# Ranks, places and silu in the routed experts of a two-layer trunk step on one core

## The chip, the cores and the metric

The kernel runs on one core of a Trainium2 chip, as one launch. The metric is the device time in microseconds (us) from start to end, as the median of three runs.

## The reference, cut to what matters

The reference is one step of a trunk of 2 layers on 384 tokens (128 of context, 256 latent) of width 1024. Each layer has a mixer (gated recurrence and three attentions) and then a routed feed-forward part. The change touches only that second part:

```python
def hier_moe(h, w_rg, w_re, w_g, w_u, w_d):
    glog = (x @ w_rg)                       # 4 group logits per token
    gsel = argmax(glog)                     # one group
    gw = softmax(glog)[gsel]
    elog_g = (x @ w_re)[..., gsel, :]       # 4 experts of that group
    top_p, top_i = top_k(softmax(elog_g), 2)
    top_p = top_p / sum(top_p)
    gate = one_hot(gsel * 4 + top_i) * (gw * top_p)
    hid = silu(x @ w_g) * (x @ w_u)         # 16 experts, 1024 -> 256
    y = (hid * gate) @ w_d                  # 256 -> 1024
```

All is float32.

## The kernel before, in words

**How a product is made.** The weights come from memory in units of 128 x 1024 floats (512 KB) that SyncE's queue loads. Each float32 product is made of three matmuls on rounded halves (line 1389 to 1391: high by high, low by high, high by low). So for each unit ScalarE makes the high half (`whi`, lines 1002 and 1010), VectorE in the experts or GpSimd in the mixer makes the low half (`wlo`, lines 1927 and 854), and TensorE then runs 6 matmuls of 512 columns. Three buffers (`CONV` = 3) of halves turn round: ScalarE may convert unit n only when TensorE has done with unit n - 3. Twelve raw buffers (`RING`) lie in front of that.

**The experts.** A token goes to one group, and its group's experts are run on tiles of 128 tokens, sorted by group through a table in memory. There are 6 tiles in a layer (`NT`), each with the 24 units (`UNITS`) of its group's four experts. For expert e, units (e, 0) to (e, 3) hold the gate and up weights and give `G`; then ScalarE takes tanh of the gate part (line 1297), and VectorE's `hidden` makes (tanh + 1) x gate part (line 2327) and multiplies by the token's routing weight and the up part (line 2331; the factor 2 of this form of silu is taken out of the weight in `route`). TensorE turns the result (line 1801), ScalarE and VectorE make its halves (`ehi`, `elo`), and units (e, 4), (e, 5) are the down projection into `S`. At the end of a tile ScalarE copies `S` to `yo` (line 1325). In tile 0 the rows of the tile are not read from memory but selected by matmul (line 1851) with a 0/1 matrix `sel` from the normalised rows `hn`. GpSimd scatters all rows to the sorted table (line 924), reads the next tile's rows (`hs`, line 940) and TensorE turns them (line 1809) after unit 18. TensorE's and VectorE's code of tiles 1 to 4 is a loop in hardware, and so is ScalarE's for tiles 0 to 4.

**The route.** `route` (line 576) is VectorE's part. After the router's logits it picks the group (`rg_dve`), and TensorE counts with two small matmuls (line 1566) each token's rank in its group and the groups' sizes (`rc_pe`). VectorE makes `sel` from that, finishes `hn` (`whole_row`), and then, between low halves of tile 0's units (`unit_low`, `rows_low`), it works out, in this order: the best two experts (`rt_dve`, to ScalarE's Exp on line 1291, back with `rt_act`), the routing weights (`gates_dve`, to the matmul on line 1831), the places in the sorted table (lines 647 to 663, `slot_dve`, to GpSimd's scatter). `tables`, run after unit 8 of tile 0, makes the numbers of the weight blocks of the last two tiles and the matrix of the last tile's places.

**TensorE around the route.** In layer 0 it also makes part of the next layer's modulation from 8 blocks, in two quads of 32 matmuls (`quad`, lines 1346 to 1352): one ahead of the ranks' matmuls and one behind. `keep_busy` issues matmuls on the identity that nothing reads (line 1446): `BUSY_RANK` of them ahead of the ranks' matmuls, `BUSY_PLACE` behind, each a pair of numbers for the two layers. Engines run their queues in order; semaphores join them.

Of the kernel before, what the change touches and what calls it, by code (L numbers as in the profile page):

```python
# [24 lines left out]
ALU = mybir.AluOpType  # L25
ACT = mybir.ActivationFunctionType
AX = mybir.AxisListType.X
# [70 lines left out]
BUSY_RANK, BUSY_PLACE = (0, 12), (11, 24)  # L98
NLOG = 20
SELECT_GATES = 3  # L100
# [189 lines left out]
def program(nc, a, out, counts):  # L290
# [4 lines left out]
    with ctx:  # L295
# [193 lines left out]
        e_tanh, e_dve, e_hid, e_pt = sg("e_tanh"), sg("e_dve"), sg("e_hid", credit=2), sg("e_pt")  # L489
# [86 lines left out]
        def route(dve, need, own, tt, whole_row, rows_low, next_mods, unit_low):  # L576
# [44 lines left out]
            for n in (1, 2):  # L621
                unit_low(n)

            prod = rw[:, :, 32:48].rearrange("p t (g e) -> p t g e", g=4)
            own(tt(prod, el.rearrange("p t (g e) -> p t g e", g=4), gsel.unsqueeze(3).to_broadcast([P, TILES, 4, 4]), ALU.mult))
            own(V.tensor_reduce(rw[:, :, 28:32], prod.rearrange("p t g e -> p t e g"), AX, ALU.add))
            rows_low(0)
            eg = rw[:, :, 28:32]
            first_max(eg, m1, sel1)
            own(V.tensor_scalar(rw[:, :, 48:52], sel1, NEG, None, ALU.mult))  # L630
            own(tt(rw[:, :, 48:52], rw[:, :, 48:52], eg, ALU.add))
            first_max(rw[:, :, 48:52], m2, sel2)
            rt_dve.of(tt(rw[:, :, 12:13], m2, m1, ALU.subtract))
            rows_low(1)
            unit_low(CONV)
            need(rt_act, 0)

            own(V.tensor_reduce(rw[:, :, 14:15], rw[:, :, 0:4], AX, ALU.add))
            own(V.tensor_scalar(rw[:, :, 15:16], rw[:, :, 4:5], 1.0, 2.0, ALU.add, ALU.mult))
            own(tt(rw[:, :, 14:15], rw[:, :, 14:15], rw[:, :, 15:16], ALU.mult))  # L640
            own(V.reciprocal(rw[:, :, 15:16], rw[:, :, 14:15]))
            own(tt(sel2, sel2, b4(rw[:, :, 4:5]), ALU.mult))
            own(tt(sel1, sel1, sel2, ALU.add))
            gates_dve.of(tt(hn[:, :, D:ROW], sel1, b4(rw[:, :, 15:16]), ALU.mult))
            unit_low(CONV + 1)
# [16 lines left out]
            own(V.tensor_scalar(rw[:, :, 13:14], slot, float(-(NT - 1) * P), None, ALU.add))  # L662
            slot_dve.of(V.tensor_scalar(slot_at[:, :].unsqueeze(2), slot, -1.0, None, ALU.add))
            need(sg_pe, 0)
            q_gate.of(V.tensor_copy(gate[:, :], O[:, 0:GRP]))
            for n in range(CONV + 2, LEAD):
                unit_low(n)
            next_mods()

            def tables():  # L670

                own(V.tensor_scalar(first, order[:, 4:4 + OVER], base[:, 1:2], None, ALU.is_ge))
# [6 lines left out]

                for t in range(TILES):  # L680
                    ins = V.tensor_scalar(sel[:, t, :], order[:, 4 + NT:4 + NT + P], rw[:, t, 13:14], None, ALU.is_equal)
                sel_dve.of(ins)

            return tables
# [140 lines left out]
        def _(pool):  # L825
# [9 lines left out]
            for l in range(layers):  # L835
# [30 lines left out]
                for s in SCHEDULE:  # L866
# [52 lines left out]
                    elif s == ("route",):  # L919
                        need(zero_out, NT)  # L920
                        pool.wait_ge(*slot_dve.at(l, 0))
                        carry()
# [52 lines left out]
        def _(act):  # L975
# [8 lines left out]
            for l in range(layers):  # L984
# [52 lines left out]
                for s in SCHEDULE:  # L1037
# [247 lines left out]
                    elif s == ("route",):  # L1285
# [4 lines left out]
                        act.wait_ge(*rt_dve.at(l, 0))  # L1290
                        rt_act.of(nc.scalar.activation(rw[:, :, 0:5], rw[:, :, 8:13], ACT.Exp))
                        rows_high(1, 0)
                    elif s == ("experts",):
                        def one_tile(i, last):
                            def tanh(e):
                                act.wait_ge(*e_unit.in_tile(l, i, UT, GATED[e]))
                                e_tanh.of(nc.scalar.activation(gact[:, e % 2, :], G[:, e % 2, 0:DEXP], ACT.Tanh, scale=0.5))
# [6 lines left out]
                            for n in range(3, UT):  # L1304
                                if n - 3 in GATED:
                                    tanh(GATED.index(n - 3))
                                high(i, n)
# [1230 lines left out]
```

## Time and profile before

| | |
|---|---|
| median of 3 runs | 1696.46 us (1696.36 to 1699.31) |
| profiled execution | 1698.88 us, its span 1697.3 us |
| TensorE busy | 1660.7 us, 98% |
| VectorE busy | 1010.2 us, 60% |
| ScalarE busy | 858.6 us, 51% |
| GpSimd busy | 647.4 us, 38% |
| experts of layer 0, layer 1 (us of the span) | from about 619 and 1453 |

Busy shares are means over the whole program. TensorE's ends are modelled, so its 98% holds small gaps; they are seen in the starts of the matmuls.

### The profile page before, as it was taken

What the parts mean: (1) busy time and instruction counts of PE and PEld (TensorE: products, weight loads), DVE (VectorE), ACT (ScalarE), POOL (GpSimd) and SP (SyncE); (2) the same over time, 40 slices, a digit from 0 to 9 for tenths busy, and PEclk for the clock granted to TensorE, in tenths of its full rate; (3) what the DMA queues carried; (4) which work ended last, traced back from release to release, by engine and by line L of the source; (5) the groups of instructions that cost most, each with busy time, mean ns of one, the idle gap of its engine ahead of it and who ended that gap; (6) DMA issues with size and microseconds to landing.
All of it is one profiled execution on the core that took longest, in us unless ns stands there. A gap on an engine that the chain in (4) does not pass through costs nothing.

```text
span 1697.3 us, 27078 instructions
## 1 busy us (share of the span) xinstructions
PE 1660.7 (98%) x10057; PEld 1342.9 (79%) x10057; DVE 1010.2 (60%) x1710; ACT 858.6 (51%) x1452; POOL 647.4 (38%) x408
## 2 busy tenths in 40 slices
PE   8999999999999999999999999999999999899998
PEld 7788887777888877777778888777788888777776
DVE  3137577563450279999851384765535314899997
ACT  2443344444532347878644334554544333487884
POOL 0644463434476621101135555543346674110102
PEclk9999999999999999999999999999999999999999
DMA  9723344253656659999865334334344654799994
GB/s 350 264 87 109 106 149 137 94 181 137 210 205 231 236 198 401 371 369 367 301 231 194 100 115 131 122 121 149 131 181 153 258 208 140 279 383 365 373 366 152
DMA packets 128110, 367.21 MB, mean 216 GB/s; under 512 B 12028, under 2 KB 42364, under 8 KB 128000
## 3 DMA queue, kind: packets, MB, share of 16 engines
q1 hardware_dynamic: 93872, 319.80, 52.3%
q10 hardware_dynamic: 27504, 21.74, 4.1%
q0 software_dynamic: 6624, 24.18, 3.8%
q8 instruction: 72, 1.18, 0.3%
q14 instruction: 38, 0.31, 0.1%
HBM read 341.71 MB, written 23.97 MB: 215 GB/s over the span
## 4 chain that ended last, share of the span: by engine, by line
PE 73%; DVE 13%; issue 5%; ACT 4%; DMA 2%; POOL 1%; SPq 1%; ACTq 0%; DVEq 0%; POOLq 0%
PE G L1389 19%; PE G L1391 17%; PE G L1390 17%; DVE wlo L1927 5%; ACT whi L1010 3%; DVE pA L1927 2%; PE T L1714 2%; PE O L1465 2%; PE O L1745 2%; PE S L1700 2%; DMA x_scratch<-pA 2%; PE S L1389 1%; DVE prob L1927 1%; PE T L1618 1%; PE S L1391 1%
## 5 line engine op out<-in xcount | busy, mean ns | idle before, releaser
L854 POOL TENSOR_TENSOR wlo<-raw,whi 128x1024 fp32r<-128x1024 f32 x198 | 488.3, 2471 | 557.5 <-ACT whi L1002 557.3
L1389 PE MATMUL G<-whi,hhi 128*128 128x512 f32 (+1 forms) x1440 | 578.7, 402 | 12.3 <-DVE wlo L1927 6.2
L1391 PE MATMUL G<-whi,hlo 128*128 128x512 f32 (+1 forms) x1440 | 557.9, 387 | 0.0
L1390 PE MATMUL G<-wlo,hhi 128*128 128x512 f32 (+1 forms) x1440 | 557.4, 387 | 0.0
L1389 PEld LDWEIGHTS G<-whi,hhi 128*128 128x128 f32 x1440 | 270.5, 188 | 91.0 <-DVE wlo L1927 21.1
L1391 PEld LDWEIGHTS G<-whi,hlo 128*128 128x128 f32 x1440 | 270.4, 188 | 57.4
L1390 PEld LDWEIGHTS G<-wlo,hhi 128*128 128x128 f32 x1440 | 271.1, 188 | 46.8
L1002 ACT ACTIVATE whi<-raw 128x1024 fp32r<-128x1024 f32 x204 | 214.7, 1054 | 99.6 <-PE G L1391 66.3
L1927 DVE TENSOR_TENSOR wlo<-raw,whi 128x1024 fp32r<-128x1024 f32 x150 | 179.7, 1220 | 6.7 <-ACT whi L1010 3.6
L1010 ACT ACTIVATE whi<-raw 128x1024 fp32r<-128x1024 f32 x144 | 152.7, 1060 | 40.7 <-PE G L1391 26.8
L1927 DVE TENSOR_TENSOR wlo<-pA,whi 128x1024 fp32r<-128x1024 f32 x72 | 88.0, 1224 | 33.2 <-ACT whi L1010 31.7
L1010 ACT ACTIVATE whi<-pA 128x1024 fp32r<-128x1024 f32 x72 | 76.5, 1063 | 36.3 <-PE S L1391 18.7
L1927 DVE TENSOR_TENSOR wlo<-pB,whi 128x1024 fp32r<-128x1024 f32 x72 | 85.6, 1224 | 7.4 <-ACT whi L1010 6.8
L1229 ACT ACTIVATE prob<-prob,am 128x384 f32<-128x384 f32 x64 | 38.9, 609 | 99.3 <-DVE am L1927 52.9
L1389 PE MATMUL S<-whi,ehi 128*128 128x512 f32 x192 | 79.4, 414 | 6.3 <-DVE elo L1927 5.9
L1010 ACT ACTIVATE whi<-pB 128x1024 fp32r<-128x1024 f32 x72 | 75.0, 1056 | 7.7 <-PE G L1391 7.1
L1389 PE MATMUL G<-whi,bhi 128*128 128x512 f32 x192 | 78.4, 408 | 0.0
L849 POOL TENSOR_TENSOR sink_col<-ones 128x1 f32<-128x1 f32 x26 | 15.7, 603 | 162.4 <-ACT yo L1325 76.7
L1391 PE MATMUL S<-whi,elo 128*128 128x512 f32 x192 | 75.4, 392 | 0.0
L1390 PE MATMUL S<-wlo,ehi 128*128 128x512 f32 x192 | 75.1, 391 | 0.0
L1391 PE MATMUL G<-whi,blo 128*128 128x512 f32 x192 | 75.1, 391 | 0.0
L1390 PE MATMUL G<-wlo,bhi 128*128 128x512 f32 x192 | 74.9, 390 | 0.0
(404 smaller groups left out, 2323.3 us busy)
## 6 DMA issues: line engine op xcount, KB each, us to landing
raw<-in_units SPq DMA_DIRECT2D x423, 512.0 KB, 5.1
pA<-in_units SPq DMA_DIRECT2D x78, 512.0 KB, 5.8
pB<-in_units SPq DMA_DIRECT2D x72, 512.0 KB, 5.9
h_sorted<-sig POOLq DMA_DIRECT2D x12, 514.0 KB, 6.9
hs<-h_sorted POOLq DMA_DIRECT2D x10, 514.0 KB, 7.4
y_sorted<-yo POOLq DMA_DIRECT2D x10, 512.0 KB, 7.0
bias<-in_nat_bias ACTq DMA_DIRECT2D x16, 256.0 KB, 3.6
pB<-rows_scratch ACTq DMA_DIRECT2D x8, 512.0 KB, 9.2
```

The lines of the kernel that those rows point to most:

```text
L854: lo_done.of(nc.gpsimd.tensor_tensor(wlo[:, k, :], raw[:, POS_OF[g] % RAW, :], whi[:, k, :].bitcast(F32), ALU.subtract))
L1002: hi_done.of(nc.scalar.activation(whi[:, g % CONV, :], raw[:, p % RAW, :], ACT.Copy))
L1010: hi_done.of(nc.scalar.activation(whi[:, n % CONV, :], expert_raw(n), ACT.Copy))
L1229: e = nc.scalar.activation(prob[:, u % 2, m, lo:lo + w], src, ACT.Exp, bias=am[:, u % 2, i:i + 1], accum_out=am[:, u % 2, 4 + i:5 + i])
L1389: nc.tensor.matmul(dst, st_hi, mv_hi, start=start, stop=False)
L1390: nc.tensor.matmul(dst, st_hi, mv_lo, start=False, stop=False)
L1391: return nc.tensor.matmul(dst, st_lo, mv_hi, start=False, stop=stop)
L1465: mm = nc.tensor.matmul(O[32 * q:32 * q + 32, c0:c0 + P], cond[:, k, :], raw[:, MODPOS[j - MQ + 1 + q] % RAW, k * P:(k + 1) * P], start=(k ...
L1700: nc.tensor.matmul(S[:, m, 0:256], q, kT[r, kj, 0:256], start=True, stop=True)
L1714: mm = nc.tensor.transpose(T[:, m, b * P:(b + 1) * P], prob[:, u % 2, m, b * P:(b + 1) * P], ident[:, :])
L1745: mm = nc.tensor.matmul(O[64 * m:64 * m + 64, to], values(b, lo, 64), pr, **fl)
L1927: return V.tensor_tensor(o, i0, i1, op)
```

## The change

It moves work inside the route, and takes silu in one operation of ScalarE.

```diff
-BUSY_RANK, BUSY_PLACE = (0, 12), (11, 24)
+BUSY_RANK, BUSY_PLACE = (0, 14), (0, 28)
-SELECT_GATES = 3
+SELECT_GATES = 4
+TABLES = (12, 15)
 # VectorE, route: new order after the ranks' sums, sel and whole_row(2)
-            for n in (1, 2):
-                unit_low(n)
-            (group's expert logits) rows_low(0) (best two experts, rt_dve)
-            rows_low(1) unit_low(CONV) need(rt_act, 0)
-            (routing weights, gates_dve) unit_low(CONV + 1)
             (places: at, tiles, base, diff, cum, slot; slot_dve)
+            unit_low(1) rows_low(0) unit_low(2)
+            (group's expert logits, best expert)
+            rows_low(1) unit_low(CONV)
+            (second expert, rt_dve) unit_low(CONV + 1) need(rt_act, 0)
-            own(V.tensor_scalar(rw[:, :, 15:16], rw[:, :, 4:5], 1.0, 2.0, ALU.add, ALU.mult))
+            own(V.tensor_scalar(rw[:, :, 15:16], rw[:, :, 4:5], 1.0, None, ALU.add))
+            (routing weights, gates_dve) unit_low(CONV + 2)
             need(sg_pe, 0)
             q_gate.of(V.tensor_copy(gate[:, :], O[:, 0:GRP]))
-            for n in range(CONV + 2, LEAD):
-                unit_low(n)
             next_mods()
 # tables: block numbers, now after unit 12 (with the slot offset of rw 13);
 # the last tile's matrix is split off as last_places, after unit 15
-                                if n == LAST_SEL and first:
-                                    tables()
+                                if n in TABLES and first:
+                                    finish_route[TABLES.index(n)]()
 # GpSimd, scatter of the rows
                         pool.wait_ge(*slot_dve.at(l, 0))
+                        pool.wait_ge(*gates_dve.at(l, 0))
 # ScalarE
                         rows_high(0, 0)
-                        act.wait_ge(*rt_dve.at(l, 0))
-                        rt_act.of(nc.scalar.activation(rw[:, :, 0:5], rw[:, :, 8:13], ACT.Exp))
                         rows_high(1, 0)
-                                e_tanh.of(nc.scalar.activation(..., G[:, e % 2, 0:DEXP], ACT.Tanh, scale=0.5))
+                                e_silu.of(nc.scalar.activation(..., G[:, e % 2, 0:DEXP], ACT.Silu))
                                 high(i, n)
+                                if n == CONV + 1 and first:
+                                    act.wait_ge(*rt_dve.at(l, 0))
+                                    rt_act.of(nc.scalar.activation(rw[:, :, 0:5], rw[:, :, 8:13], ACT.Exp))
-                        with act.Fori(0, NT - 1) as i:
-                            one_tile(i, False)
-                        one_tile(NT - 1, True)
+                        for i in range(NT):
+                            one_tile(i, i == NT - 1, i == 0)
 # TensorE, route
                         if l < DEPTH - 1:
-                            quad(0)
+                            quad(0, range(KD // 2))
                         keep_busy(S[:, 1, 0:P], BUSY_RANK[l])
                         need(rg_dve, 0)
                         (the ranks' two matmuls, rc_pe)
                         if l < DEPTH - 1:
+                            quad(0, range(KD // 2, KD))
                             quad(1)
                         keep_busy(S[:, 1, 0:P], BUSY_PLACE[l])
 # VectorE, hidden
-                                dve.wait_ge(*e_tanh.in_tile(l, i, GRP, e))
+                                dve.wait_ge(*e_silu.in_tile(l, i, GRP, e))
-                                e_dve.of(V.scalar_tensor_tensor(ga_, ga_, 1.0, b[:, 0:DEXP], ALU.add, ALU.mult))
-                                dve.wait_ge(*e_dve.in_tile(l, i, GRP, e))
```

Lines in brackets stand for statements that are the same before and after, moved as they are. `SELECT_GATES` is the unit of tile 0 after which TensorE makes the tile's routing weights.

## Rows read from the trace of the kernel before

**Rows 1.** Windows: two stretches of the experts; busy us (x instructions) by engine, clock, DMA.

```profile
648.00:662.00 14.00, 13.69 (x65) 10.83 (x65) 13.18 (x16) 10.81 (x15) 2.29 (x3) 1.00 1.03 410
699.00:735.50 36.50, 35.91 (x161) 28.11 (x160) 33.77 (x39) 29.17 (x36) 4.30 (x6) 1.00 0.98 375
```

**Rows 2.** Chain of waits through tile 2 of layer 0: start us, us, what.

```profile
699.28 0.44 ACT yo L1325
...
710.84 0.43 DVE sig L2327
711.68 1.23 DVE wlo L1927
712.96 0.50 PE G L1389
...
735.92 0.44 ACT yo L1325
```

**Rows 3.** Timeline of TensorE in tile 2: start us, us, engine, line, operation.

```profile
712.50 0.39 PE L1391 MATMUL S<-whi,elo 128*128 128x512 f32 x1
...
730.97 0.39 PE L1390 MATMUL S<-wlo,ehi 128*128 128x512 f32 x1
731.20 0.39 PE L1391 MATMUL S<-whi,elo 128*128 128x512 f32 x1
731.91 0.49 PE L1389 MATMUL S<-whi,ehi 128*128 128x512 f32 x1 [0.32 <-DVE elo L1927]
```

**Rows 4.** Timeline of VectorE in tile 2.

```profile
731.37 0.41 DVE L1927 TENSOR_TENSOR elo<-T,ehi 128x256 fp32r<-128x256 f32 x1
```

**Rows 5.** Groups of instructions by line, ScalarE: busy, mean ns, idle before.

```profile
L1297 ACT ACTIVATE sig<-G 128x256 f32<-128x256 f32 x48 | 18.4, 384 | 18.4 <-PE G L1391 18.4
```

**Rows 6.** Timeline, layer 0, from the ranks' sums to unit 8 of tile 0.

```profile
609.45 0.17 DVE L612 COPY rw<-O 128x12 f32<-128x12 f32 x1 [1.02 <-PE O L1566]
...
612.24 2.35 DVE L1927 TENSOR_TENSOR wlo<-pA,whi 128x1024 fp32r<-128x1024 f32 x2
...
613.78 2.84 PE L1851 MATMUL T<-prob,hn 128*128 128x128 f32 x24
...
619.28 0.48 PE L1389 MATMUL G<-whi,hhi 128*128 128x512 f32 x1
...
629.97 0.50 PE L1389 MATMUL G<-whi,hhi 128*128 128x512 f32 x1 [2.22 <-DVE wlo L1927]
...
636.55 0.50 PE L1389 MATMUL S<-whi,ehi 128*128 128x512 f32 x1 [1.44 <-DVE elo L1927]
```

**Rows 7.** Timeline of VectorE, layer 0: first and last of the places' 15 operations.

```profile
625.89 0.16 DVE L648 TENSOR_SCALAR rw<-rw 128x4 f32<-128x4 f32 x1
...
628.55 0.17 DVE L663 TENSOR_SCALAR slot_at<-rw 128x3 int32<-128x3 f32 x1
```

**Rows 8.** Timeline of TensorE, layer 1, the same stretch.

```profile
1442.00 5.60 PE L1446 MATMUL S<-ident 128*128 128x128 f32 x48
1447.44 2.84 PE L1851 MATMUL T<-prob,hn 128*128 128x128 f32 x24
...
1452.72 0.47 PE L1389 MATMUL G<-whi,hhi 128*128 128x512 f32 x1
...
1470.06 0.50 PE L1389 MATMUL S<-whi,ehi 128*128 128x512 f32 x1 [1.44 <-DVE elo L1927]
```

**Rows 9.** Windows: three us after the router's logits of layer 0.

```profile
605.50:608.50 3.00, 3.00 (x64) 2.91 (x56) 2.72 (x10) 0.00 (x0) 0.00 (x0) 0.50 0.02 5
```

**Rows 10.** Timeline of ScalarE in the mixer: a table load and its user.

```profile
928.02 1.28 ACT L1199 ACT_TABLE_LOAD   x1
931.87 1.28 ACT L1199 ACTIVATE prob<-prob,ms 128x128 f32<-128x128 f32 x4 [2.57 <-DVE ms L2179]
```

**Rows 11.** Timeline, tile 0 of layer 0: the next tile's rows asked for, and turned.

```profile
643.72 0.60 POOL L940 DMA_DIRECT2D hs<-h_sorted  x1
...
652.93 0.60 PE L1809 MATMUL T<-ident,hs 128*128 128x128 f32 x4
```

More of the change, by code:

```diff
@@ L488, in program @@
         e_unit, e_lo = sg("e_unit", credit=RAW), sg("e_lo", credit=RAW)
-        e_tanh, e_dve, e_hid, e_pt = sg("e_tanh"), sg("e_dve"), sg("e_hid", credit=2), sg("e_pt")
+        e_silu, e_hid, e_pt = sg("e_silu"), sg("e_hid", credit=2), sg("e_pt")
         e_hh, e_hl = sg("e_hh"), sg("e_hl", credit=1)
@@ L620, in route @@
             whole_row(2)
-            for n in (1, 2):
-                unit_low(n)
[L624 to L638, printed above, removed]
-            own(V.tensor_scalar(rw[:, :, 15:16], rw[:, :, 4:5], 1.0, 2.0, ALU.add, ALU.mult))
[L640 to L645, printed above, removed]
             at = order[:, 4:4 + GRP]
@@ L678, in tables, with last_places @@
                                                 first.unsqueeze(2), float(RAW * k), None, ALU.add))
+            def last_places():
                 for t in range(TILES):
@@ L682, in tables @@
                 sel_dve.of(ins)
-            return tables
+            return tables, last_places
         block = ctx.enter_context(nc.Block())
@@ L1289, in _, with one_tile, silu @@
                         rows_high(0, 0)
-                        act.wait_ge(*rt_dve.at(l, 0))
-                        rt_act.of(nc.scalar.activation(rw[:, :, 0:5], rw[:, :, 8:13], ACT.Exp))
                         rows_high(1, 0)
                     elif s == ("experts",):
-                        def one_tile(i, last):
-                            def tanh(e):
+                        def one_tile(i, last, first=False):
+                            def silu(e):
                                 act.wait_ge(*e_unit.in_tile(l, i, UT, GATED[e]))
-                                e_tanh.of(nc.scalar.activation(gact[:, e % 2, :], G[:, e % 2, 0:DEXP], ACT.Tanh, scale=0.5))
+                                e_silu.of(nc.scalar.activation(gact[:, e % 2, :], G[:, e % 2, 0:DEXP], ACT.Silu))
                             def turned_hid(e):
@@ L1305, in one_tile @@
                                 if n - 3 in GATED:
-                                    tanh(GATED.index(n - 3))
+                                    silu(GATED.index(n - 3))
                                 high(i, n)
+                                if n == CONV + 1 and first:
+                                    act.wait_ge(*rt_dve.at(l, 0))
+                                    rt_act.of(nc.scalar.activation(rw[:, :, 0:5], rw[:, :, 8:13], ACT.Exp))
                                 if n - 3 in TURN_HID:
@@ L1344, in _, with next_quad @@
             pe.wait_ge(cond_dve, 2)
-            def next_quad(q, where, signal):
-                for k in range(KD):
+            def next_quad(q, where, signal, ks=range(KD)):
+                for k in ks:
                     for i in range(MQ):
@@ L1391, in three, with quad @@
                     return nc.tensor.matmul(dst, st_lo, mv_hi, start=False, stop=stop)
-                def quad(q):
+                def quad(q, ks=range(KD)):
                     need(nx_in[q], MQ - 1)
-                    next_quad(q, home, nx_pe.of)
+                    next_quad(q, home, nx_pe.of, ks)
                 def turned():
@@ L2318, in _ @@
                     elif s == ("route",):
-                        tables = route(dve, need, own, tt, whole_row, lambda hf: rows_low(hf, 0), next_mods,
+                        finish_route = route(dve, need, own, tt, whole_row, lambda hf: rows_low(hf, 0), next_mods,
                                        lambda n: unit_low(0, n))
```

26 lines of the change are left out of this document (24 added, 2 removed).

## The prediction

> **What bounds the kernel now.** I read the page first (TensorE 98% busy, VectorE at nine tenths in the experts), then windows of the experts, then the chain of waits through one tile, then the timeline of the engines where the chain leaves TensorE. In tile 2 of layer 0 [rows 1] VectorE is busy 33.8 of 36.5 us, ScalarE 29.2, and TensorE's 35.9 holds gaps that only its starts show. Tile 2 takes 36.64 us from one `yo` copy to the next (735.92 - 699.28) [rows 2]. Matmuls that wait for nothing start 0.23 us apart (730.97 to 731.20) [rows 3], so a unit of six is 1.38 us and 24 units 33.1 us; with the turns of `hid` and `hs` about 34.6. So some 2 us of each tile are waits for halves. Only three buffers of halves turn round, so what ScalarE and VectorE spend in a row at one unit reaches TensorE. The chain shows it: VectorE's line 2327 (0.43) stands ahead of a low half, and TensorE starts that unit at 712.96 [rows 2] though it could have gone on at 712.50 + 0.23 = 712.73 [rows 3]. At 731.20 + 0.23 = 731.43 it waits to 731.91 for `elo`, at the end of an unbroken row on VectorE (731.37 plus 0.41) [rows 3, 4].
>
> Tile 0 is worse: between unit 0 and unit 8 pass 17.27 us in layer 0 (619.28 to 636.55) [rows 6] and 17.34 in layer 1 [rows 8], where 8 x 1.38 and about 0.85 for two small extra steps would make 11.9. The two largest waits are 2.22, for a low half behind the places' operations, and 1.44, for the `elo` behind `tables` [rows 6, 7]. Ahead of it, VectorE waits 1.02 for the ranks' sums in layer 0, and TensorE starts the selection at 613.78 although `hn` was ready at about 612.3, where the low halves follow (612.24, with an overlap of 0.08); `keep_busy` holds its queue [rows 6].
>
> **Part 1, silu in one operation: tiles 1 to 5.** Removed are 48 operations of line 2327 with the wait between two of VectorE's own, 0.43 to 0.44 each by the chain [rows 2]: four in a tile. What stays is line 2331. ScalarE's Silu replaces a Tanh of the same 128 x 256 (384 ns [rows 5]). The trace has no Silu. Its nearest row is that Tanh, so I take 0.38; the lower bound is the same, the upper is two passes, 0.77 (a rival). Of the three waits that the removed operation feeds, the one at 712.73 is 0.23 and then 0.10 of a slower first matmul; the same pattern comes at expert 2; the `elo` wait at 731.43 is 0.48 plus 0.10. Together 1.2. The operation's 0.44 covers the first two and nearly all of the third. Left as they are: the wait behind the `yo` copy (about 0.4) and the one for expert 0's `elo` (0.2), which hang on the way TensorE, ScalarE, VectorE and not on VectorE's queue. I take 1.0 a tile; bounds 0.5 (next in line is ScalarE's way, which has only some 0.15 to spare per unit: 2 x 1.38 against 0.27 + 1.09 + 1.28) and 1.3. Tiles 1 to 4 in two layers: 8.0 (4 to 10.4). The last tile has no next rows and shows under 0.3 of such waits: 0.2 each, 0.4. A tile then takes 35.6.
>
> **Part 2, the head of layer 0.** The half quad ahead of the ranks takes 8 of 16 groups, so TensorE is free at about 607.0 instead of 608.7 (at half clock, 0.50 in this stretch [rows 9], which is the 1.2 GHz level; TensorE ran the router's 20-column matmuls just before). The group is known at 607.1, so the sums come at about 608.0, before VectorE has ended its `whole_row` at 608.4. Its wait of 1.02 is gone [rows 6], and `hn` is ready at 611.2. TensorE's remaining 24 groups end at 610.9, no `keep_busy` follows, and the selection starts at 611.3: 2.5 earlier than 613.78. Unit 0 follows 5.5 later as before, at 616.8. VectorE meanwhile does the places: one less than the 15 operations of 2.66 + 0.17 [rows 7], so to 613.9. Low half 1 (1.13 apart, from 2.35 for two [rows 6]) and `rows_low(0)` end at 615.6, low half 2 at 616.7. All are in time.
>
> **Units 0 to 8.** I walk VectorE's queue with 0.19 for each small operation ((628.55 - 625.89) / 14 [rows 7]). Low half 3 needs unit 0 done (618.2, then 0.27 + 1.06 + 0.1): it ends at 620.7. Eight small operations: 622.2; this is `rt_dve`. Low half 4: 623.4, while TensorE was free at 622.3: wait 1.1. The Exp (now behind ScalarE's high half 4) is back by 622.5 and delays high half 5 to 623.8, which nobody yet needs. Seven operations (the weights): 624.7, low half 5: 625.9; TensorE ends unit 4 and the small matmul at 625.5: wait 0.4. Two copies and line 2331: 626.7, low half 6: 627.8; TensorE free at 627.4: wait 0.4. Low halves 7, 8 and `elo`: 630.4; units 6 and 7 end at 630.7. So unit 8 starts at 630.7, 13.9 after unit 0 instead of 17.27: 3.4 gained. `tables` and `last_places` come after units 12 and 15 instead of 8, some 2.0 us on VectorE. What hides them is the time that the removed line 2327 gives there (0.44 each) and VectorE's half us without work near unit 13; of the rest I count 1.0 as a new wait, which takes back tile 0's own 1.0 to 1.2 of part 1. Layer 0, tile 0: 2.5 + 3.4 = 5.9; bounds 3 (walk 1.5 off, selection held 1.4 by something else) and 7.
>
> **Layer 1.** `BUSY_RANK` 12 to 14 adds four passes: 0.4 on the way to the ranks. `BUSY_PLACE` 24 to 28 adds 8 passes of 5.44 / 48 = 0.113 [rows 8]: 0.9. The selection starts 1.3 later. VectorE is not late for it (places done near 1448.0, the selected rows come at 1452.3). Then the same 13.9 instead of 17.34: 3.4 less. Net 2.1; bounds 0 and 3.5.
>
> **Part 3, what is added to ScalarE.** Exp and Tanh share a table in the trace, and Silu needs another if it is not in it, so up to three more loads: one ahead of each layer's first Silu, one back at layer 1's first Exp. A load takes 1.28 and is issued ahead of its user's wait: it starts at 928.02 while the Exp waits to 931.87 [rows 10]. In tile 0 it would run from 623.8 to 625.1, Silu and high half 6 behind it end by 626.5, and VectorE reaches that half at 626.7. Hidden, with 0.2 to spare. In layer 1's prologue it fits in ScalarE's wait for `lam`. I count 0 for all three; without that cover it is 1.3 each.
>
> The Trainium skill (ScalarE: Activation LUTs, What ACT_TABLE_LOAD costs) speaks against this part: it puts every switch at about 2.66 us, of which 1.38 is a drain, and asks to batch calls by set. The trace has the 1283 ns of the load and shows no drain ahead of it there; by that figure the sum would be some 3 us less.
>
> GpSimd's scatter waits for the weights too: at 624.7 it starts 3.9 earlier in layer 0 and 0.3 earlier in layer 1. SyncE's and GpSimd's DMAs are the same in number. The ScalarE loop is unrolled: it showed no gap at its turn (I count 0).
>
> **Sum.** 8.0 + 0.4 + 5.9 + 2.1 = 16.4 us. Against the profiled execution: 1698.9 - 16.4 = 1682.5 (span 1697.3 to 1680.9). That execution lies 2.4 above the median of the runs shown, so the forecast for the median is 1696.5 - 16.4 = 1680.1.
>
> **Rivals.**
> 1. The tiles don't get shorter because memory sets their pace. For: the DMA share is 0.98 at 375 GB/s [rows 1]. Against: 410 GB/s at 648 to 662, so a tile's 13.6 MB needs 33.2 us, and ScalarE's waits in tile 2 name TensorE, not a DMA. Then only the heads gain, 8.0: 1688.5. Chance 0.10.
> 2. The next tile's rows come late. They are asked for at 643.72 and turned at 652.93 [rows 11], about 9 us with some 1.8 to spare. TensorE gets there 5 earlier, the request only 3.9; in layer 1 it is 1.2 against 0.3. If the scatter, now among denser loads, slips by 2 to 3, the heads' gain is cut by 2 to 5 in all: 1682 to 1686. Chance 0.12.
> 3. ScalarE pays for each switch more than the load. In tile 0 high half 6 is then 1.4 later, minus the 0.2 to spare, in both layers, and layer 1's prologue loses 1: 3.4 in all, 1683.5. Against: no drain shows beside the load [rows 10]. By the rule of the Trainium skill (ScalarE: Activation LUTs, What ACT_TABLE_LOAD costs) it would come out so. Chance 0.08.
> 4. Less filler lets the clock fall again: one more stretch at 0.50 [rows 9] of the same 3.4 us in each layer costs 1.7 each: 1683.5. TensorE has no gap over 1.2 in the new tile 0, where before it had 2.2 without a fall. Chance 0.06.
> 5. Slower than before: Silu is done in two passes, 0.77. It stands at ScalarE ahead of a high half at each expert, where little is to spare, so TensorE gets 0.39 more at each of 48: 18.7 against 16.4 gained, 1698.8. It decides from a Silu of about 0.72 on. For it: nothing but that the trace has none. Chance 0.04.
> 6. The order doesn't do what it says (the walk above is too short and unit 4 to 8 wait as long as before, and tiles gain half): 5 gained, 1691.5. Chance 0.05.
>
> **How the numbers follow.** The forecast has 0.55: 1680.1, its own range 1676 to 1685. The range adds the bounds: all low ends of the terms give 7 us (1689.5), all high ends 21.7 (1674.8); rivals 1 to 4 lie inside. I give 1674 to 1689.5. A measurement of this kernel tells about 0.2% (3.4 us) from no change; cases 1 to 4 and most of 6 are faster by more: 0.90. Same 0.05, slower 0.05.
>
> **What would show it.** Right: 35.6 us between `yo` copies, VectorE 32.0 busy in a tile, no line 2327, Silu 0.38; the selection near 611.3 and unit 8 near 630.7 in layer 0, 1448.8 and 1467.9 in layer 1 minus what layer 0 gained; six to eight table loads of 1.28, none on the chain. Wrong: tiles of 36.6 with ScalarE waiting for DMAs; a wait of TensorE ahead of line 1809; a clock of 0.50 behind the selection; a Silu over 0.5.

## The result, and the profile after

The changed kernel takes 1683.45 us (median of 5 runs, 1681.85 to 1686.77). Its ratio to the kernel before is 0.991, with an interval of 0.9893 to 0.9926: 0.9% faster. (The ratio goes by all the runs and not by the two medians, which are 13.0 us or 0.8% apart.) The forecast was 1680.1, with a range of 1674 to 1689.5. The profiled execution took 1682.95 (span 1681.4), where the one of before took 1698.88 (span 1697.3): 15.9 less, against 16.4 in the sum of the prediction.

The page of after: TensorE's share stays at 98%, VectorE has 48 operations less, and in the chain of waits VectorE's share falls from 13% to 7% while TensorE's rises from 73% to 83%.

```profile
span 1681.4 us, 26841 instructions
...
PE 1653.9 (98%) x10047; PEld 1340.6 (80%) x10047; DVE 996.6 (59%) x1662; ACT 862.5 (51%) x1455; POOL 644.5 (38%) x408
...
PE 83%; DVE 7%; DMA 3%; issue 3%; ACT 2%; POOL 1%; SPq 1%; POOLq 0%; ACTq 0%; DVEq 0%
```

Line numbers have moved by a few: the unit's three matmuls are lines 1392 to 1394 (before 1389 to 1391), the low halves line 1931 (1927), the selection line 1855 (1851), the turn of the next rows line 1813 (1809), the `yo` copy line 1330 (1325), Silu line 1299 (Tanh was 1297).

Groups by line, ScalarE (busy, mean ns, idle before). One Silu costs what one Tanh did [rows 5], 385 ns, and the tables are loaded twice for it; all table loads of the kernel are of 1283 ns.

```profile
L1299 ACT ACTIVATE sig<-G 128x256 f32<-128x256 f32 x48 | 18.5, 385 | 17.3 <-PE G L1394 17.3
...
L1299 ACT ACT_TABLE_LOAD x2 | 2.6, 1283 | 0.0
```

The chain through tile 2 of layer 0, which answers to [rows 2]. From one `yo` copy to the next pass 730.05 - 694.27 = 35.78 us in place of 36.64. The first `G` unit behind the `S` units, which waited behind line 2327 (712.96 in [rows 2]), starts at 707.75, 0.23 us after the matmul ahead of it, and there the chain no longer leaves TensorE.

```profile
694.27 0.35 ACT yo L1330
...
696.25 1.24 DVE wlo L1931
697.54 0.50 PE G L1392
...
704.90 0.49 PE S L1392
705.39 0.23 PE S L1393
...
707.68 0.23 PE S L1394
708.14 0.23 PE G L1393
...
730.05 0.35 ACT yo L1330
```

Timeline of TensorE, layer 0, from the selection to unit 8 [rows 6]. Unit 0 follows the selection by 5.60; units 0 to 8 take 632.12 - 617.89 = 14.23 in place of 17.27. The waits of 2.22 and 1.44 are gone; one of 1.07 stands at unit 4, then 0.16 and 0.30.

```profile
612.29 2.94 PE L1855 MATMUL T<-prob,hn 128*128 128x128 f32 x24
...
617.89 0.48 PE L1392 MATMUL G<-whi,hhi 128*128 128x512 f32 x1
...
624.74 0.47 PE L1392 MATMUL G<-whi,hhi 128*128 128x512 f32 x1 [1.07 <-DVE wlo L1931]
...
629.26 0.50 PE L1392 MATMUL G<-whi,hhi 128*128 128x512 f32 x1 [0.30 <-DVE wlo L1931]
...
632.12 0.39 PE L1392 MATMUL S<-whi,ehi 128*128 128x512 f32 x1
```

The same of layer 1 [rows 8]: 13.90 in place of 17.34. Behind it TensorE waits 0.43 for a low half that stands behind the tables, and 0.33 for the next tile's rows, the wait of rival 2.

```profile
1438.77 2.84 PE L1855 MATMUL T<-prob,hn 128*128 128x128 f32 x24
...
1444.05 0.47 PE L1392 MATMUL G<-whi,hhi 128*128 128x512 f32 x1
...
1457.95 0.39 PE L1392 MATMUL S<-whi,ehi 128*128 128x512 f32 x1
...
1465.93 0.51 PE L1392 MATMUL G<-whi,hhi 128*128 128x512 f32 x1 [0.43 <-DVE wlo L1931]
...
1475.34 0.66 PE L1813 MATMUL T<-ident,hs 128*128 128x128 f32 x4 [0.33 <-DMA hs<-h_sorted]
```

Windows ahead of layer 0's selection: busy by engine, then the granted clock, DMA share and GB/s. The first answers to [rows 9]. TensorE is at 0.50, its 1.2 GHz level, in both; the stretch at 0.50 is 6.8 us long, that of before was 3.4.

```profile
605.50:608.50 3.00, 3.00 (x47) 2.49 (x41) 2.74 (x13) 0.00 (x0) 0.00 (x0) 0.50 0.03 5
608.50:611.50 3.00, 3.00 (x64) 2.79 (x60) 2.83 (x12) 0.00 (x0) 0.00 (x0) 0.50 0.00 0
```

### The profile page after: what moved, and what is told of

Same layout as the page of the kernel before. It is cut to its first block, busy times and chain, and to the rows that moved or that the text cites. A ratio compares the mean times of both kernels' runs of the same rounds, so it can differ in the third digit from the quotient of the medians.

```text
span 1681.4 us, 26841 instructions
## 1 busy us (share of the span) xinstructions
PE 1653.9 (98%) x10047; PEld 1340.6 (80%) x10047; DVE 996.6 (59%) x1662; ACT 862.5 (51%) x1455; POOL 644.5 (38%) x408
## 4 chain that ended last, share of the span: by engine, by line
PE 83%; DVE 7%; DMA 3%; issue 3%; ACT 2%; POOL 1%; SPq 1%; POOLq 0%; ACTq 0%; DVEq 0%
PE G L1392 20%; PE G L1394 18%; PE G L1393 18%; PE S L1392 3%; PE S L1394 3%; PE S L1393 3%; DVE pA L1931 2%; PE T L1718 2%; PE O L1468 2%; DVE wlo L1931 2%; PE O L1749 2%; PE S L1704 2%; DMA x_scratch<-pA 2%; DVE prob L1931 1%; PE T L1622 1%
```

## The experiments

Each kernel ran in 5 rounds (4 to 12 runs) beside the kernel before, on the same chip. There were four such batches on four chips, in which the kernel before had medians of 1696.85 to 1699.34 us: across batches the ratios are compared, not the us. The traces are of one execution each. "Tile" is the median time between `yo` copies in tiles 1 to 4, "units 0 to 8" and "rest" are the two parts of tile 0 (from unit 0 to 8, from there to the first `yo` copy), for layer 0 / layer 1. The last column is the length of the stretch with TensorE's granted clock at 0.50 that ends ahead of the selection of layer 0 / 1 in the profiled execution. (e1_silu has its one stretch of 3.4 us later, at 1455.7, inside layer 1's 17.55; e10_pieces has one more of 3.4 at 11.2.)

```
kernel          us       ratio   interval          tile         units 0-8     rest          0.50 us
before          1696.46  -                         36.67        17.27/17.34   26.06/26.12   3.4/3.4
after           1683.45  0.991   0.9893 to 0.9926  35.81        14.23/13.90   26.30/26.77   6.8/0
e1_silu         1686.37  0.9935  0.9916 to 0.9954  35.79        16.99/17.55   25.95/26.08   0/0
e2_route        1695.93  0.9994  0.9982 to 1.0006  36.92        14.28/14.11   27.28/27.28   10.2/6.8
e3_fill12       1679.52  0.9894  0.9874 to 0.9915  35.77        14.22/13.86   26.27/26.32   3.4/0
e4_nosplit      1682.28  0.9903  0.9884 to 0.9921  35.78        14.20/13.88   26.31/27.25   10.2/0
e5_unroll       1700.15  1.0018  1.0009 to 1.0028  36.91        17.26/17.34   26.27/26.28   3.4/6.8
e6_rolled       1684.74  0.992   0.9905 to 0.9935  35.66        14.22/13.88   26.36/26.73   6.8/6.8
e7_silu_twice   1693.34  0.9976  0.9965 to 0.9986  36.76        14.22/13.88   26.56/27.42   6.8/3.4
e9_switch       1714.81  1.0095  1.0079 to 1.0112  38.3, 39.8   14.25/13.88   26.32/26.91   6.8/3.4
e8_narrow       1683.23  0.992   0.9903 to 0.9937  35.62        13.99/13.66   26.01/27.66   3.4/3.4
e10_pieces      1677.04  0.9874  0.986 to 0.9889   35.62        14.23/13.85   25.95/26.76   6.8/3.4
e11_later       1677.98  0.9884  0.987 to 0.9899   35.63        13.13/13.16   26.81/27.07   6.8/3.4
e12_fill11      1681.21  0.9902  0.9883 to 0.9922  35.61        14.20/13.88   27.46/26.33   6.8/3.4
```

**The two halves of the change: e1_silu and e2_route.** e1_silu is the kernel before with Silu alone (and ScalarE's tiles written out):

```diff
-   e_tanh.of(nc.scalar.activation(gact[...], G[...], ACT.Tanh, scale=0.5))
+   e_tanh.of(nc.scalar.activation(gact[...], G[...], ACT.Silu))
-   e_dve.of(V.scalar_tensor_tensor(ga_, ga_, 1.0, b[:, 0:DEXP], ALU.add, ALU.mult))
```

> The kernel before with silu alone (Silu on ScalarE, line 2327 and its wait gone, ScalarE's tiles unrolled, the factor 2 gone); the route as before. Theory: the tiles gain by VectorE's shorter queue whatever the route does: tiles 1 to 4 take 35.8 us from yo to yo (36.65 before), tile 0 gains 1.2 in each layer (its waits of 1.44, 0.35 and 0.4 all shrink by the 0.44 of the operation), so 6.6 + 0.4 + 2.4 = 9.4 us faster than before, 1687. Rival: the tile gain needs the new order of tile 0 (denser loads, less backlog); then tiles stay at 36.6 and the gain is under 3, 1694.

e2_route is the reverse: the changed kernel with Tanh and line 2327 back, so the new order (and the written-out tiles) alone.

> The kernel after with tanh and line 2327 back (factor 2 back); the new route, fillers and split quad stay. Theory: 6.5 us faster than before, 1690: tile 0 gains about 1.6 a layer net of the tables' waits (which line 2327's absence no longer hides), the heads 1 to 2, and tiles 1 to 4 stay at 36.65. Rival: the new order is worth nothing without silu, because the tables' two pieces meet line 2327 in units 12 to 16: then 1695 to 1697.

Measured: e1_silu is at 0.9935 with tiles of 35.79, as its theory had it (only the 1.2 us that it gave each tile 0 came out smaller). e2_route is at 0.9994, with 1 in its interval, where 6.5 us less than before had been expected. It did take 3.0 and 3.2 us out of units 0 to 8, but the rest of tile 0 is 1.2 longer in both layers, and the tiles are 36.92 long.

That does not make the new order worthless. Both kernels, like the changed one, have ScalarE's tiles written out, and e5_unroll (below) shows that this alone costs 0.18%. With e5_unroll there are the four cases of silu and order, all with tiles written out:

```
                     old order            new order
Tanh, line 2327      1.0018 (e5_unroll)   0.9994 (e2_route)
Silu                 0.9935 (e1_silu)     0.991  (after)
```

Silu gives 0.0083 in the old order and 0.0084 in the new, some 14 us. The new order gives 0.0024 with Tanh, where the intervals lie apart, and 0.0025 with Silu, where they overlap a little: some 4 us. The two gains add up; no run shows that the halves of the change need each other.

The traces agree on the tables, which moved from units 0 to 8 into the rest of tile 0. With Tanh the rest is 1.0 longer in both layers (27.28 in e2_route, 26.27 and 26.28 in e5_unroll). With Silu it is 26.30 and 26.77 after the change; e1_silu has 25.95 and 26.08, but of these 0.71 and 0.87 are waits for the next tile's rows, where the changed kernel waits 0 and 0.33. Without these waits the tables cost 1.06 and 1.2, as much as with Tanh, and Silu by itself saves about 1.0 of the rest. These two cancel.

```profile
650.10 0.66 PE L1807 MATMUL T<-ident,hs 128*128 128x128 f32 x4 [0.71 <-DMA hs<-h_sorted]
```

**Written-out tiles on ScalarE: e5_unroll and e6_rolled.** e2_route's tiles, 0.26 longer than before with the same work in them, asked for this pair. e5_unroll is the kernel before, e6_rolled the changed kernel, with the loop exchanged:

```diff
 e5_unroll
-  with act.Fori(0, NT - 1) as i:
-      one_tile(i, False)
-  one_tile(NT - 1, True)
+  for i in range(NT):
+      one_tile(i, i == NT - 1)
 e6_rolled
-  for i in range(NT):
-      one_tile(i, i == NT - 1, i == 0)
+  one_tile(0, False, True)
+  with act.Fori(1, NT - 1) as i:
+      one_tile(i, False)
+  one_tile(NT - 1, True)
```

> The kernel before with one edit: ScalarE's five expert tiles are written out instead of four turns of a loop and one written out; Tanh, the scalar_tensor_tensor behind it and the order stay. It tells apart what made the tiles of e2_route 36.9 us where the kernel before has 36.65 with the same work in a tile. Theory A (the written-out tiles on ScalarE cost it): tiles 36.9, 8 x 0.25 = +2.0 us, 1698.9. Theory B (it comes from the new order or from the table loads in the tiles' first): tiles 36.65 and 1696.9 +- 0.7.

> The changed kernel with one edit: ScalarE's tiles 1 to 3 are three turns of a loop instead of written out. If written-out tiles cost 0.25 us each, three tiles in two layers give back 6 x 0.25 = 1.5 us: tiles 1 to 3 at 35.55, 1681.9. If they cost nothing: tiles 35.8 and 1683.4 +- 1.

(The loop of e6_rolled has four turns, tiles 1 to 4, not the three that I wrote; so it is 8 tiles. The same holds for e8_narrow and the later kernels with that loop.) Two `yo` copies in a row, first of e5_unroll (36.92 apart, 36.64 before), then of e6_rolled (35.64 apart, 35.78 after):

```profile
698.91 1.01 ACT L1325 ACTIVATE yo<-S 128x1024 f32<-128x1024 f32 x1
735.83 1.01 ACT L1325 ACTIVATE yo<-S 128x1024 f32<-128x1024 f32 x1
```

```profile
694.31 1.00 ACT L1330 ACTIVATE yo<-S 128x1024 f32<-128x1024 f32 x1
729.95 1.01 ACT L1330 ACTIVATE yo<-S 128x1024 f32<-128x1024 f32 x1
```

Written out, ScalarE's tiles cost 0.25 us each beside the Tanh form, and the time shows it (ratio 1.0018, interval above 1). In the changed kernel they cost 0.15 each, 1.2 us in eight tiles, by the traces. The ratios of e6_rolled and after (0.992 and 0.991) don't show this, and their intervals overlap widely; the profiled execution of e6_rolled was at 0.50 for 6.8 us more ahead of layer 1's selection than that of after. Why the written-out form is slower isn't settled; no single wait in tile 2 grows by more than 0.1.

**What the chain is worth, and where it ends: e7_silu_twice and e8_narrow.** The first adds to ScalarE's part of the chain unit, silu, hidden product, turn. The second shortens VectorE's part; it leaves out 248 of the product's 256 columns, so its output is not the kernel's. Both edits reach all 48 silus or products, not the 40 of the expectations:

```diff
 e7_silu_twice, ahead of each Silu
+   e_dup.of(nc.scalar.activation(gact[:, 2, :], G[:, e % 2, 0:DEXP], ACT.Silu))
 e8_narrow (and the loop of e6_rolled)
-   e_hid.of(V.scalar_tensor_tensor(hid[:, e % 2, :], ga_, gate[:, e:e + 1], b[:, DEXP:], ...))
+   e_hid.of(V.scalar_tensor_tensor(hid[:, e % 2, 0:8], ga_[:, 0:8], gate[:, e:e + 1], b[:, DEXP:DEXP + 8], ...))
```

> The changed kernel with every Silu of the experts done twice, the first time into a spare 128x256 area: 40 more operations of 385 ns on ScalarE, each between TensorE's unit and the hidden product, so each adds its time to the same chain from which the change took 0.43 to 0.48 us. My theory (that chain sets the wait at each expert's end, and 0.21 us of each 0.4 taken from it came back to TensorE): +0.2 per expert, tiles 36.6, 1683.5 + 40 x 0.2 = 1691.5, about where the price of a Silu with two passes was put. Rival (the changed kernel has no slack left, so each 0.385 us counts whole): tiles 37.35, 1699. Rival (after the change that chain has room): under 1685.

> e6_rolled (the changed kernel with ScalarE's tiles 1 to 3 in a loop) with the hidden product of each expert done for 8 of its 256 columns, the rest of it left out: 40 operations on VectorE of 0.16 instead of 0.48 us, in the same chain from unit to turned hidden rows. By the price that e7_silu_twice gave (0.96 us of a tile for 4 x 0.385 on the chain, 0.62 of each us) the tiles would fall by 4 x 0.32 x 0.62 = 0.8 from 35.65 to 34.85, 1678. Theory: less, since TensorE waits only 0.9 us in a tile of the changed kernel and two of these four waits are at the tile's turn, behind other work: 35.2, 1681. Rival (TensorE's own work is the bound by now): 35.6, 1684.

Four extra Silus of 0.385 in a tile make it 0.95 longer (36.76 against 35.81): 0.62 of each us added reaches TensorE, about as the theory had it (36.6 and 1691.5). Four hidden products 0.32 shorter make it no shorter: 35.62 against 35.66. My theory fell, and the number of the rival held. Groups by line of e8_narrow in tile 2: the first matmul of a unit has 0.1 us of idle time ahead of it in all, and ScalarE's waits name TensorE, not a transfer, although the DMA share is 1.00 there.

```profile
L1395 PE MATMUL G<-whi,hhi 128*128 128x512 f32 x33 | 13.3, 402 | 0.1
...
L1395 PE MATMUL S<-whi,ehi 128*128 128x512 f32 x16 | 6.6, 414 | 0.0
```

```profile
L1014 ACT ACTIVATE whi<-raw 128x1024 fp32r<-128x1024 f32 x12 | 12.7, 1060 | 2.0 <-PE G L1397 1.1 <-PE S L1397 0.8
L1014 ACT ACTIVATE whi<-pA 128x1024 fp32r<-128x1024 f32 x7 | 7.4, 1064 | 2.4 <-PE S L1397 1.8 <-PE G L1397 0.6
```

But TensorE's ends are modelled, so small gaps are seen only in the starts. By these, three units of the tile still start late in e8_narrow, by 0.30, 0.12 and 0.13 over the 0.23 of an unhindered matmul, each followed by 0.10 of a slower first matmul: about 0.9 in all. Two of the three:

```profile
694.78 0.40 PE L1397 MATMUL G<-whi,hlo 128*128 128x512 f32 x1
695.31 0.50 PE L1395 MATMUL G<-whi,hhi 128*128 128x512 f32 x1
...
723.26 0.39 PE L1397 MATMUL S<-whi,elo 128*128 128x512 f32 x1
723.62 0.49 PE L1395 MATMUL S<-whi,ehi 128*128 128x512 f32 x1
```

So the matmuls of a tile, one behind the other, take about 34.7 us, near the 34.6 of the prediction, and 35.6 is what is left when VectorE's queue no longer holds anything back. The rest are the wait behind the `yo` copy and two for `elo`; they are the same in e6_rolled (0.30, 0.12, 0.12) and did not shrink with the product. The kernel before lay 1.05 above 35.6, the changed one 0.2, and with the loop 0.05. That also tells why the removed operation's 4 x 0.44 = 1.76 us gave 1.0 a tile and no more: what VectorE's queue had held back was used up.

**The price of a table switch: e9_switch.** An Exp of 128 x 8 ahead of the second expert's Silu. The condition takes in tile 5 too, so it is ten Exps and 20 loads, not the eight and 16 of the expectation:

```diff
+   if e == 1 and i:
+       e_dup.of(nc.scalar.activation(gact[:, 2, 0:8], G[:, e % 2, 0:8], ACT.Exp))
```

> The changed kernel with an Exp of 128x8 into a spare area ahead of the second expert's Silu in tiles 1 to 4 of each layer, so that ScalarE loads its tables twice there, once for the Exp and once again for the Silu: 16 loads of 1.28 us. The Exp's load can stand ahead of its wait, the Silu's can't. Theory A (a load costs its 1.28 us and nothing more): 1.28 + 0.2 for the Exp into the chain of one expert in each of 8 tiles, of which the other experts' half rate takes some away: tiles 1 to 4 longer by 0.8 to 1.5, 1690 to 1695. Theory B (a switch costs a further drain of about as much again, as the Trainium skill has it in ScalarE: Activation LUTs, What ACT_TABLE_LOAD costs): idle time beside each load, tiles longer by 2.8 or more, 1706.

Timeline of ScalarE in tile 2, then TensorE's wait behind it:

```profile
706.48 1.06 ACT L1015 ACTIVATE whi<-raw 128x1024 fp32r<-128x1024 f32 x1 [0.26 <-PE G L1399]
707.56 1.28 ACT L1303 ACT_TABLE_LOAD   x1
708.85 0.18 ACT L1303 ACTIVATE sig<-G 128x8 f32<-128x8 f32 x1
709.05 1.28 ACT L1304 ACT_TABLE_LOAD   x1
710.34 0.38 ACT L1304 ACTIVATE sig<-G 128x256 f32<-128x256 f32 x1
```

```profile
712.98 0.50 PE L1397 MATMUL G<-whi,hhi 128*128 128x512 f32 x1 [2.21 <-DVE wlo L1936]
```

The loads take 1.28 each and follow their neighbours within 0.02 us: 2.78 from the first load to the Silu, of which 2.47 came into tiles 1 and 3 (and 2.3 and 2.4 into the last tiles). No drain shows, so theory B's mechanism is refuted; but theory A's size was wrong too, because the first load was hardly covered: the `whi` ahead of it ended at 707.54, and the last matmul of TensorE's unit started at 707.36. The Trainium skill (ScalarE: Activation LUTs, What ACT_TABLE_LOAD costs) has 2.66 us for each switch. Here two switches and an Exp took 2.78; the two differ, and the measurement decides.

Most of the surplus over that is the clock. Tiles 2 and 4 are 39.8 long and 1 and 3 are 38.3, with the same wait of 2.2 in each (712.98 above; 752.81 in tile 3). In tiles 2 and 4 a stretch at 0.50 of 3.4 us follows it:

```profile
714.00:717.40 3.40, 3.40 (x10) 2.51 (x9) 2.38 (x3) 1.06 (x1) 0.00 (x0) 0.51 0.82 263
717.40:720.80 3.40, 3.40 (x17) 2.88 (x16) 2.04 (x4) 2.61 (x4) 0.00 (x0) 0.99 0.86 334
```

That gives a price: one such stretch costs 39.83 - 38.27 = 1.56 us in full expert work. With the switches and four such stretches the kernel takes 1714.81 us, more than either theory had.

**TensorE ahead of the selection: e3_fill12, e4_nosplit, e12_fill11.** e3_fill12 has 12 filler matmuls for 28 ahead of layer 1's selection (the trace shows each as two passes); e4_nosplit has the whole quad ahead of the ranks' sums; e12_fill11 is e10_pieces (below) with 11 fillers back ahead of layer 0's selection.

```diff
 e3_fill12
-BUSY_RANK, BUSY_PLACE = (0, 14), (0, 28)
+BUSY_RANK, BUSY_PLACE = (0, 14), (0, 12)
 e4_nosplit
-    quad(0, range(KD // 2))
+    quad(0)
...
-    quad(0, range(KD // 2, KD))
 e12_fill11
-BUSY_RANK, BUSY_PLACE = (0, 14), (0, 12)
+BUSY_RANK, BUSY_PLACE = (0, 14), (11, 12)
```

> The kernel after with BUSY_PLACE of layer 1 at 12 instead of 28. Theory: in layer 1 the selection waits for filler alone: VectorE ends hn and the places by 1438.0 and idles 3.1 us; with 12 the selection starts 3.2 us earlier (when hn is ready) and unit 0 and the rest follow 2.5 to 3.1 earlier: 1680.7 for a median of 1683.4. Rival: the filler keeps TensorE's clock; with 16 fewer the granted clock falls to 0.5 for 3.4 us or more in layer 1 and the time is the same or up to 1.7 longer, 1683 to 1685.

> The kernel after with the whole first quad ahead of the ranks, as before the change. Theory: the split is worth little, since TensorE and not VectorE sets the start of the selection in layer 0 (24 or 16 groups behind the ranks end at the same time): VectorE waits 1.0 to 1.7 for the sums again, but ends hn at 611.8 when the quads end at 612.1: 0 to 0.7 slower than after. Rival: the start of the ranks sets all that follows and 1.0 to 1.7 is lost, 1684.5 to 1685.

> e10_pieces with the 11 filler matmuls that the kernel before had ahead of layer 0's selection put back. The kernels with them and the old order (the kernel before, e1_silu, e5_unroll) had the granted clock at 0.50 for 3.4, 0 and 3.4 us ahead of that selection, those without them for 3.4, 6.8 or 10.2 us. Theory (the fillers, or more work on TensorE in that stretch, bring the clock back earlier): one stretch of 3.4 or none, selection at 611.5 to 612.0 in place of 612.71, 1676.5. Rival (the fall starts at 603 to 607, ahead of the fillers, and its length does not hang on them): 6.8 us again, the fillers add 0.5 to 1.2: 1678.

Layer 1 of e3_fill12: the selection starts 3.48 after the ranks' matmuls instead of 6.70 and now waits 0.19 for VectorE's `hn`. The 32 passes less are worth 3.2 us in the profile, and the clock doesn't fall in the units behind, so the theory held. (The medians, 1683.45 and 1679.52, agree with that, but their intervals overlap.)

```profile
1434.71 2.94 PE L1855 MATMUL T<-prob,hn 128*128 128x128 f32 x24 [0.19 <-DVE hn L1973]
```

Layer 0's selections are best counted from the quad's first matmul (605.26 before, 604.74 after, 604.40 in e3_fill12), since the work ahead of it is the same in every kernel, and yet it ends up to 3.1 us apart. From there the selection follows after 8.52 us in the kernel before and 7.55 after the change. In e3_fill12, where the stretch at 0.50 was 3.4 us as before, it is 6.78, at 611.18.

e4_nosplit is the same as after (0.9903 against 0.991, intervals nearly equal), so the split quad is worth nothing that can be measured. Its profiled execution was at 0.50 for 10.2 us, like that of e2_route, which has the split: in both the selection follows the quad's start by 8.11 us. The ranks' matmuls come 1.7 us later without the split, and nothing is lost by it, as the theory had it.

In e12_fill11 the stretch is 6.8 long, the selection starts 8.91 after the ranks' matmuls (5.61 in e10_pieces), and the ratio is 0.9902 where e10_pieces has 0.9874; the two intervals just touch. The fillers can't have ended the stretch: they stand behind the quads, and the stretch (606.7 to 613.5) was over 0.2 us after they began. They run at full clock and take 2.67 us, where my rival had 0.5 to 1.2; the other 0.6 of the 3.3 is the quads, which end that much later (613.26 against 612.71).

```profile
613.26 2.84 PE L1455 MATMUL S<-ident 128*128 128x128 f32 x22
615.93 2.84 PE L1861 MATMUL T<-prob,hn 128*128 128x128 f32 x24
```

The next tile's rows are 1.44 late in it as well.

**A faster version: e10_pieces and e11_later.** e10_pieces joins e3_fill12 and e6_rolled and runs the tables in three pieces:

```diff
-TABLES = (12, 15)
+TABLES = (15, UT - 1, UT + 2)
-            return tables, last_places
+            return last_places, firsts, indices
```

> A version meant to be faster: 12 filler matmuls in place of 28 ahead of layer 1's selection, ScalarE's tiles 1 to 3 in a loop, and the first tile's tables in three pieces (the last tile's places behind unit 15's low half, the rest behind units 23 and 26 where VectorE waits for ScalarE anyway). From e3_fill12's 1679.5: six tiles 0.15 shorter = -0.9, and TensorE's waits of 0.42 and 0.43 behind the tables gone = -0.8: 1677.8. Rival (the pieces only move the wait to the tile's turn, and written-out code is no cost beside the clock's spread): 1679.5.

e11_later moves unit 3's low half behind four of the small operations that followed it:

```diff
-            unit_low(CONV)
             own(V.tensor_scalar(rw[:, :, 48:52], sel1, NEG, None, ALU.mult))
...
+            unit_low(CONV)
```

> e10_pieces with the low half of unit 3 put four small operations later in the routing on VectorE, into the 0.85 us in which it waited for ScalarE's high half (at 619.6 in e3_fill12). If VectorE's own work is what makes TensorE wait at units 4 to 6 (1.07 + 0.15 + 0.32), these waits fall by 0.8 in each layer and it takes 1.6 off e10_pieces. Rival (unit 3 comes late by the same time and the next units follow it): the same as e10_pieces within 0.3.

e10_pieces has the lowest ratio of all: 1677.04, 0.9874 (0.986 to 0.9889), whose interval lies below that of the change. It overlaps with those of e3_fill12 and e11_later, so what the loop and the three pieces add to the 12 fillers is not shown by the time. In layer 0 the rest of tile 0 fell from 26.27 to 25.95 (the wait behind the tables, 0.42, didn't go: 0.44 of it stands at a later unit, so this much the rival had right); in layer 1 it rose from 26.32 and stands at 26.76, because the next tile's rows now come 0.69 late. e11_later shows the same in both layers. Unit 4's wait fell from 1.07 to 0.26 and units 0 to 8 to 13.13 / 13.16, 1.1 and 0.7 less; the rest grew by 0.86 and 0.31, and the time is that of e10_pieces, as the rival had it:

```profile
622.25 0.47 PE L1402 MATMUL G<-whi,hhi 128*128 128x512 f32 x1 [0.26 <-DVE wlo L1941]
...
646.71 0.65 PE L1823 MATMUL T<-ident,hs 128*128 128x128 f32 x4 [0.73 <-DMA hs<-h_sorted]
```

```profile
1470.33 0.66 PE L1823 MATMUL T<-ident,hs 128*128 128x128 f32 x4 [0.99 <-DMA hs<-h_sorted]
```

GpSimd asks for those rows when its scatter has landed, at 641.20 after the change (643.72 before, [rows 11]). Where the rows are late, tile 0 is thus bounded by the path weights, scatter, load, turn: most of what is gained ahead of the turn is handed back at it.

## Why the prediction was right, and where it was off

By the profiled executions, with forecast and measured side by side ("last tile" is tile 5, from the `yo` copy of tile 4 on):

```
step                                     forecast   measured
selection of layer 0                      -2.5       -1.5
units 0 to 8 of layer 0                   -3.4       -3.0
rest of tile 0, layer 0 / layer 1         0 / 0      +0.2 / +0.7
tiles 1 to 4, layer 0 / layer 1           -4.0/-4.0  -3.4 / -3.5
last tile to layer 1's ranks' sums        +0.2       -2.0
from there to the selection of layer 1    +0.9       +0.9
units 0 to 8 of layer 1                   -3.4       -3.4
last tile of layer 1 and the end          -0.2       -1.0
sum (+0.1 from selection to unit 0)       -16.4      -15.9
```

*The mechanism of the tiles was right.* VectorE's queue set the waits at units and at `elo`, and without line 2327 they are gone, but for 0.14 of the 0.48 at `elo`. e8_narrow shows that 35.6 us is what is left, the length that the prediction gave a tile, with the waits of 0.4 and 0.2 that it left as they were (0.41 and 0.22 in e8_narrow, the slower first matmul counted in). Its 1.0 a tile was exact where ScalarE's loop stays (e6_rolled, 36.67 to 35.66).

*The first step that was mis-sized is "The ScalarE loop is unrolled ... I count 0".* It costs 0.15 a tile here, 1.2 in all (e5_unroll, e6_rolled). That is the whole difference in the rows of tiles 1 to 4.

*The second is the last tile, "0.2 each, 0.4".* It got 0.87 and 0.98 shorter (34.89 to 34.02 and 34.94 to 33.96), 1.85 in all. The prediction saw under 0.3 of waits there; by the starts of the matmuls before the change, 0.11, 0.26 and 0.36 stood ahead of three units, and all are gone. This is the whole last row of the table: from the last `yo` copy to the end pass 19.5 us before and after, although the stretch at 0.50 there is shorter after the change. With the loop's 1.2 it nearly cancels.

*The selection of layer 0* missed 611.3 by 1.0. Counted from the quad's first matmul the route gained 1.0 and not 2.5; the other 0.5 of the row came from work ahead of the change. With a stretch of 3.4 us as before it gains 1.7 (e3_fill12), so the walk was too short by 0.8 even then, and its 611.18 is near 611.3 by luck: its quads had begun 0.9 earlier. The further 0.8 is the longer stretch of the profiled execution, 6.8 us (five more kernels with 6.8 took 7.15 to 7.91 from the quad's start to the selection, the two with 3.4 took 6.76 and 6.78). So rival 4's extra stretch did come in layer 0, at some half of its 1.7. That the missing filler brought it is not shown: the 11 fillers stand behind the quads, and e12_fill11, which has them, shows 6.8 us too.

*The row of -2.0* is made of -0.9 in the last tile, +0.4 for four more passes, as forecast, and -1.5 for a stretch at 0.50 in layer 1 that the execution of before had and that of after had not. e1_silu bears this out: it has the old fillers and no stretch there, and takes 1.6 less than before from the last `yo` copy to the sums (596.5 against 598.1). That 15.9 comes so close to 16.4 is therefore in part luck: the selection, units 0 to 8, the rest of tile 0 and the loop fell short by some 3.4 us, and the last tiles and this stretch gave 2.9 back.

Executions of one kernel differ by such stretches: the four of e10_pieces had a mean granted clock of 0.998, 0.998, 0.997 and 0.996 and took 1675.7, 1675.8, 1678.3 and 1679.6 us. The medians are 13.0 apart where the profiled executions are 15.9, since that of before lay 2.4 above its median and that of after 0.5 below. The prediction took the whole sum off the median as well, and missed it by 3.4.

*The walk through units 0 to 8* held: the wait of 1.1 at unit 4 stands at 1.07 in the trace, and the total is 14.23 and 13.90 for 13.9. Only the later waits came out smaller (0.16 and 0.30 for 0.4 and 0.4).

*The tables* came as forecast: a new wait of 1.0, which takes back what Silu saves in the rest of tile 0. The runs show 1.0 to 1.2 for the tables, with Silu or without, and about 1.0 for Silu (the four cases above). In layer 1 the late rows of rival 2 add 0.3.

*The table loads* cost nothing, rivals 3 and 5 fell: 624.67 is the load ahead of the first Silu, between `whi` and the Silu at 625.97, and VectorE's product isn't late for it. e9_switch shows the same load in full where nothing covers it, and no drain.

*What the prediction did not say* is that the new order is worth some 4 us and Silu some 14, the written-out tiles left aside (by its terms, with the tables' 2 x 1.0 taken from the order, they would be 6.0 and 10.4), and that 16 of the 28 matmuls of `BUSY_PLACE` only delay layer 1's selection, by 3.2 us (e3_fill12). The step from 24 to 28 was in the sum, 0.9, and came as forecast.

*The range*: the high ends of the terms, as they are given, add up to 21.3 and not 21.7, so the lower bound would be 1675.2; it changes nothing in the range stated.

## What to carry to other kernels

Count the small costs on every engine of a change, the form of a loop too: 0.15 us in each of eight tiles was counted as 0 here, and the sum came out near only because other terms erred the other way. Compare a part of a change with a kernel that shares its side effects: e2_route beside the kernel before looked worthless, beside e5_unroll it is worth 4 us. Where an operation is taken out of a chain, work out the next bound first (here the 35.6 us of a tile): it says how much of the removed time can come back, and when to stop. Where work is moved out of one stretch, look for the cover in the stretch that takes it, and for the transfer that the earlier arrival will now wait for.

## What was not expected of the hardware

The stretches at the lower clock come in lengths of 3.4, 6.8 and 10.2 us, in the same place of kernels that do the same there: ahead of layer 0's selection, 3.4 in e3_fill12, 6.8 in e10_pieces, 10.2 in e4_nosplit. TensorE runs matmuls that move 20 columns just ahead of it, and in it matmuls on weights of 32 columns. What a stretch costs hangs on where it lies: 1.56 us for 3.4 in full expert work, 0.4 to 1.1 for 3.4 more ahead of the selection, and nothing that shows at the end of the kernel. In e9_switch the same wait of 2.21 us was followed by one in every second tile only. What decides whether it comes, and how long it lasts, stays open.

```profile
604.40:614.40 10.00, 10.00 (x142) 8.71 (x142) 6.15 (x25) 0.24 (x1) 0.06 (x1) 0.50 0.03 8
```

The row is of e4_nosplit: ten us at 0.50 with TensorE busy throughout.
